# Hybrid attention/DeltaNet backbone, 1 core: attention in 32 units of two maps, products in halves of the array, seven modulation pairs moved into the first FFN

## What is computed

```python
s = einsum('bqhmd,bthmd->bhmqt', dq, dk) * 64**-0.5     # 4 differential heads, 2 maps each
p = softmax(s)
a = p[:, :, 0] - lam * p[:, :, 1]
d_out = rms_norm(einsum('bhqt,bthe->bqhe', a, dv), subln_g) * (1 - lam_init)
s = einsum('bqgrd,btgd->bgrqt', gq, gk) * 64**-0.5      # 8 grouped heads: 2 key heads, 4 queries each
g_out = einsum('bgrqt,btgd->bqgrd', softmax(s), gv)
y = concat(d_out, g_out) @ w_out
```

## Time and profile before

| | us |
|---|---|
| median of 3 runs | 1403.09 (1401.18 to 1406.2) |
| the profiled execution | 1406.29 |
| its span, first to last instruction | 1404.2 |
| mean granted TensorE clock | 0.939 of full |

### The profile page before, as it was taken

The page is one execution under the profiler, slowest core; times in us unless marked ns, Lnnn a source line. Parts: engine busy times, 40 slices in busy tenths (PEclk is TensorE's granted clock), DMA queues, the critical chain, the costliest instruction groups (busy, mean ns, idle before and its releaser), DMA issues.

```text
span 1404.2 us, 19657 instructions
## 1 busy us (share of the span) xinstructions
PE 1243.1 (89%) x7965; PEld 1013.4 (72%) x7965; DVE 664.8 (47%) x1016; ACT 573.0 (41%) x1003; POOL 183.4 (13%) x170
## 2 busy tenths in 40 slices
PE   5699989998949999999999579968758977999996
PEld 3377755566828888888888258867657966999996
DVE  2433257554373232333222564559955556555444
ACT  2322246444343222323222346555374635444542
POOL 0120320100041111111000310010011432111101
PEclk9899999999969999999999779988967999999998
DMA  7555555775303333333333112223101214466661
GB/s 280 180 166 152 163 165 180 240 255 151 90 15 91 90 105 91 100 95 88 93 107 87 36 45 71 66 75 93 29 1 41 54 31 120 138 186 186 172 182 40
DMA packets 239140, 159.63 MB, mean 114 GB/s; under 512 B 14522, under 2 KB 213580, under 8 KB 239052
## 3 DMA queue, kind: packets, MB, share of 16 engines
q1 hardware_dynamic: 238272, 158.10, 38.0%
q10 hardware_dynamic: 780, 0.29, 0.1%
HBM read 157.32 MB, written 1.05 MB: 113 GB/s over the span
## 4 chain that ended last, share of the span: by engine, by line
PE 76%; DVE 13%; ACT 5%; issue 2%; DMA 2%; POOL 1%; ACTq 0%; SPq 0%; DVEq 0%; POOLq 0%
PE bank L1331 55%; PE bank L1319 3%; PE bank L1456 2%; PE bank L1479 2%; PE bank L1370 2%; DVE w_lo L1736 2%; DVE h_lo L1783 1%; DVE xT L1806 1%; PE bank L1464 1%; PE bank L1301 1%; DVE blocks L995 1%; PE bank L754 1%; DVE outer L993 1%; DVE conv_out L1071 1%; DVE h_hi L1782 1%
## 5 line engine op out<-in xcount | busy, mean ns | idle before, releaser
L1331 PE MATMUL bank<-h_hi,w_hi 128*128 128x512 f32 (+2 forms) x1240 | 442.9, 357 | 63.5 <-DVE h_lo L1783 33.9
L1331 PE MATMUL bank<-h_lo,w_hi 128*128 128x512 f32 (+2 forms) x1240 | 434.7, 351 | 0.0
L1331 PE MATMUL bank<-h_hi,w_lo 128*128 128x512 f32 (+2 forms) x1240 | 434.2, 350 | 0.0
L1736 DVE TENSOR_TENSOR w_lo<-w_raw,w_hi 128x1024 fp32r<-128x1024 f32 (+1 forms) x203 | 249.8, 1232 | 307.1 <-ACT w_hi L1540 306.4
L1331 PEld LDWEIGHTS bank<-h_hi,w_hi 128*128 128x128 f32 (+1 forms) x1240 | 242.2, 195 | 105.5 <-issue 63.9
L1331 PEld LDWEIGHTS bank<-h_hi,w_lo 128*128 128x128 f32 (+1 forms) x1240 | 242.6, 196 | 29.7 <-issue 1.0
L1331 PEld LDWEIGHTS bank<-h_lo,w_hi 128*128 128x128 f32 (+1 forms) x1240 | 243.1, 196 | 27.0 <-issue 0.5
L1540 ACT ACTIVATE w_hi<-w_raw 128x1024 fp32r<-128x1024 f32 (+1 forms) x203 | 209.7, 1037 | 102.0 <-PE bank L1331 84.6
L1331 PE MATMUL bank<-act_hi,w_hi 128*128 128x512 f32 (+1 forms) x352 | 118.3, 336 | 0.0
L1331 PE MATMUL bank<-act_lo,w_hi 128*128 128x512 f32 (+1 forms) x352 | 118.3, 336 | 0.0
L1331 PE MATMUL bank<-act_hi,w_lo 128*128 128x512 f32 (+1 forms) x352 | 118.3, 336 | 0.0
(11 more groups left out here) (252 smaller groups left out, 1432.1 us busy)
## 6 DMA issues: line engine op xcount, KB each, us to landing
w_raw<-in_ada_w SPq DMA_DIRECT2D x96, 512.0 KB, 4.9
w_raw<-in_ffn_w_gate_up SPq DMA_DIRECT2D x88, 512.0 KB, 3.8
w_raw<-in_ffn_w_down SPq DMA_DIRECT2D x32, 512.0 KB, 4.0
w_raw<-in_gdn_w_in SPq DMA_DIRECT2D x32, 512.0 KB, 4.0
w_raw<-in_attn_w_in SPq DMA_DIRECT2D x14, 512.0 KB, 3.9
w_raw<-in_ffn_w_down SPq DMA_DIRECT2D x16, 384.0 KB, 3.3
w_raw<-in_attn_w_out SPq DMA_DIRECT2D x8, 512.0 KB, 4.9
w_raw<-in_gdn_w_out SPq DMA_DIRECT2D x8, 512.0 KB, 5.8
```

Of the source, the lines that this page charges most:

```text
L1331: m = nc.tensor.matmul(dst, stationary(a, k), moving(b, k), start=(first and k == kk[0] and a == b == 0), stop=(last and k == kk[-1] and a ...
L1736: nc.vector.tensor_tensor(w_lo[where[key] % N_RAW][:, 0:tiles, 0:w], raw_slot(key)[:, 0:tiles, 0:w], w_hi[m % N_SPLIT][:, 0:tiles, 0:w].bi ...
```

## The change

1. `ATT_UNITS` has 32 units, one of 8 tiles of 128 features and a block of 128 queries, each with two maps. Tiles 0 to 3 are the differential heads. Tiles 4 to 7 hold one grouped head of each key head.
2. `scores` gives each map the 64 rows of its own half: rows 0 to 63 and rows 64 to 127 of the array, into two banks. `q_sb` is no longer doubled, and POOL writes each query tile once.
3. `values` of a grouped tile puts each map's 64 value columns in its own half of the array's columns; the values are no longer doubled, and one copy takes the whole 128 partitions.
4. Attention has a ring of six banks ("att") and one bank for outputs ("out"); `o_stat` stays in "work".
5. Of the 31 modulation pairs 24 stay in attention (in every step but those with qb = 0), and 7 go behind the gate chunks n = 1, 3, ... 13 of the FFN of layer 0.
6. `SPLIT_OUT_AT` is n = 32, behind the last unit. Each chunk of the output projection comes in three DMAs, which sort its rows to the new order of heads.

```diff
-ATT_UNITS = [(head, qb) for head in range(DIFF_HEADS + GQA_HEADS) for qb in range(T // P)]
+ATT_UNITS = [(tile, qb) for tile in range(KT) for qb in range(T // P)]
...
+def key_tile(tile):
+    return 1 + tile if tile < DIFF_HEADS else 0
+
+
+def turned_maps(tile):
+    return range(1 if tile < DIFF_HEADS else 2)
...
-    if phase == "att" and step % 3 and ATT_PAIR[step] < 31:
-        return pair(34, ATT_PAIR[step])
+    if phase == "att" and step % 4:
+        return pair(34, step - step // 4 - 1)
+    if phase == "gate0" and step % 2 and step < 14:
+        return pair(82, step // 2)
...
-        q_sb = at("q_sb", [KT, 2, T], F32, BIG)
+        q_sb = at("q_sb", [KT, T], F32, BIG)
...
+        RINGS = {"work": (2, 3, 4, 5, 6), "side": (7, 1), "att": (2, 3, 4, 5, 6, 1), "out": (7,), "extra": (0, 7, 1), "core": (2, 3, 4, 5, 6, 7, 1, 0)}
...
                 for n in range(2 * FT):
                     project(("gate", layer, n), ("gate", layer, n), lo, i if n == 0 else None)
+                    ada(ada_after(f"gate{layer}", n))
...
             def scores(n):
...
+                tile, qb = ATT_UNITS[n]
+                if qb == 0:
+                    pe.wait_ge(qk_out, 5 + tile + 1)
+                dsts = [take(("s", n, m), "att") for m in range(2)]
+                for m in range(2):
+                    half = slice(m * HEAD, (m + 1) * HEAD)
+                    finish(nc.tensor.matmul(dsts[m][:, 0:keys_of(qb)], q_sb[half, tile, qb * P:(qb + 1) * P],
+                                            k_sb[half, key_tile(tile), 0:keys_of(qb)], start=True, stop=True),
+                           ("s", n, m))
...
             def turn(n):
...
+                for m in turned_maps(tile):
+                    dst = take(("t", n, m), "att")
+                    for t in range(keys_of(qb) // P):
+                        last = nc.tensor.transpose(dst[:, t * P:(t + 1) * P],
+                                                   probs[:, n % 3, m, t * P:(t + 1) * P], ident)
+                    finish(last, ("t", n, m))
...
             def values(n):
...
+                for t in range(tiles):
+                    if tile < DIFF_HEADS:
...
+                    for m in range(2):
+                        c0 = DIFF_HEADS * P + m * HEAD
+                        last = nc.tensor.matmul(dst[m * HEAD:(m + 1) * HEAD, qb * P:(qb + 1) * P],
+                                                v_sb[:, t, c0:c0 + HEAD], probsT[:, n % 2, m, t, :],
+                                                start=(t == 0), stop=(t == tiles - 1))
...
             def normalize(n):
...
-                if maps == 1:
-                    first.then_inc(probs_ready, 1)
+                if tile >= DIFF_HEADS:
+                    nc.vector.tensor_scalar(p[:, 1, :], p[:, 1, :], stats[:, n % 4, 5:6], None,
+                                            ALU.mult).then_inc(probs_ready, 1)
                     return
...
-                        for half in range(2):
-                            last = nc.gpsimd.tensor_scalar(q_sb[:, u - 5, half, :], qk_n[:, u % 3, :],
-                                                           tab[:, C_HALF + half:C_HALF + half + 1], one,
-                                                           ALU.mult, ALU.mult)
+                        last = nc.gpsimd.tensor_scalar(q_sb[:, u - 5, :], qk_n[:, u % 3, :], HEAD ** -0.5, None,
+                                                       ALU.mult)
...
+                elif key[0] == "attout":
+                    rest = attn_w_out[0][DIFF_HEADS * P:, key[1] * P:(key[1] + 1) * P]
+                    sp.dma_start(slot[:, 0:DIFF_HEADS, :],
+                                 columns(attn_w_out[0][0:DIFF_HEADS * P, :], key[1] * P)).then_inc(done, 16)
+                    for g in range(GQA_KV):
...
-SPLIT_OUT_AT = len(ATT_UNITS) - 4
+SPLIT_OUT_AT = len(ATT_UNITS)
```

More of the change, by code:

```diff
@@ L185, in stream @@
         for n in range(2 * FT):
-            out += [("gate", layer, n)]
+            out += [("gate", layer, n)] + [("ada", a) for a in ada_after(f"gate{layer}", n)]
         for m in range(KT):
@@ L1298, in turn_rows @@
                 pe.wait_ge(rows_ready, group + 1)
-                dst = take(("mod", group))
+                dst = take(("mod", group), "att" if group in ATT_GROUPS else "work")
                 for k in range(ADA_WIDTH // P):
@@ L1472, in values @@
                 if qb == 0:
-                    take(("o", head), "side")
-                dst = bank(("o", head))
-                wait_evacuated(pe, ("t", n))
-                c0 = head * P if head < DIFF_HEADS else 512 + (head - DIFF_HEADS) // 4 * P
+                    take(("o", tile), "out")
+                dst = bank(("o", tile))
+                for m in turned_maps(tile):
+                    wait_evacuated(pe, ("t", n, m))
                 tiles = keys_of(qb) // P
                 for t in range(tiles):
-                    m = nc.tensor.matmul(dst[:, qb * P:(qb + 1) * P], v_sb[:, t, c0:c0 + P],
-                                         probsT[:, n % 2, t, :], start=(t == 0), stop=(t == tiles - 1))
-                finish(m, ("v", n))
-                done_at[("o", head)] = jobs[0]
+                    if tile < DIFF_HEADS:
+                        last = nc.tensor.matmul(dst[:, qb * P:(qb + 1) * P], v_sb[:, t, tile * P:(tile + 1) * P],
+                                                probsT[:, n % 2, 0, t, :], start=(t == 0), stop=(t == tiles - 1))
+                        continue
+                    for m in range(2):
[3 more added lines that the diff above has]
+                                                start=(t == 0), stop=(t == tiles - 1))
+                finish(last, ("v", n))
+                done_at[("o", tile)] = jobs[0]
             for n in range(len(ATT_UNITS) + 4):
@@ L1883, in maxima @@
             def maxima(n):
-                head, qb = ATT_UNITS[n]
-                for m in range(len(maps_of(head))):
+                qb = ATT_UNITS[n][1]
+                for m in range(2):
                     wait_product(dve, ("s", n, m))
@@ L2092 @@
 LAST_QKV = ("qkv",) + QKV_STEPS[-1]
[L2093 removed]
+ATT_GROUPS = range(8, 20)
+SPLIT_OUT_AT = len(ATT_UNITS)
 SUBLN_AT = [4 * h + 7 for h in range(DIFF_HEADS)]
```

108 lines of the change are left out of this document (39 added, 69 removed).

## The result

The changed kernel takes 1391.21 us, the median of four runs (1388.32 to 1392.17), against 1404.64 for the kernel before (four runs, 1401.18 to 1406.68). The ratio is 0.9903 with a 95% interval of 0.9877 to 0.993, which leaves out 1: faster, by 1% or 13.4 us, where 1386.0 was forecast and the range was 1374 to 1400.

A forecast was written before the change was run, and what follows sets the result against it. PE was taken to bound the grouped heads and FFN, a fixed chain partly the differential heads. Terms -2.2, -1.3, -31.7, +5.3 and +12.6 sum to -17.3 us: 1389.0 profiled, 1386 median, range 1374 to 1400.

The forecast's parts named there:

- Do halves overlap: PE array: row and column halves overlap; a 64-row score pair takes 0.86 us (512 keys), a 64-column values pair 0.22.
- A change of shape, 0.11 us: PE, between products of different shape: each change costs 0.11 us, with bounds of 0.05 and 0.2.
- Start, -2.2: Start to first o_stat, 27.9 us before: query tiles written once save 1.7 us on POOL, faster scores 0.5.
- First to third o_stat, -1.3: Differential heads, 30.8 us before: the fixed chain of 6.33 us stays, each period takes 14.75 us.
- Third o_stat to last scores, -31.7: Grouped heads, 90.9 us before: four units take 14.2 us of PE work plus 0.5 of waits; 59.2 us in all.
- The end, +5.3: Attention's end, 7.6 us before: three ACT splits add 3.0 us, copies 1.2, a second maximum and exponential 1.1.
- The FFN, +12.6: FFN of layer 0: seven modulation pairs add 8.3 us, four turn_rows 3.5, a wait for DVE's copy 0.8.
- DVE and ACT: Rival, grouped heads: DVE and ACT become the bound, four units take 17 us, 9 more in all: 1395; chance 0.15.
- Passes in program order: Rival, PE: pairs of scores take three passes, +8 us: 1394; chance 0.06.
- no overlap: Rival, PE: the halves don't overlap at all, so +12.3 us: 1415; chance 0.05.
- The clock: Rival, attention: PE's waits make the clock fall again, some 3.5 us each, two falls: 1393; chance 0.07.
- more gain: Rival: the start doesn't fall to the low clock and the splits find room in ACT's waits: 1378; chance 0.12.

The follow-up runs named there:

- e1: Changed kernel with score products back on all 128 rows, each query tile written twice by POOL with one half zeroed: 1395.08 us.
- e2: Changed kernel with grouped values issued one column half after the other, not alternating: 1394.45 us.
- f4: Changed kernel with the differential heads' scaling one step later and scores on all 128 rows (e5 + e1): 1392.60 us.
- e4: Changed kernel with one output projection chunk split at attention's last step, not three: 1389.83 us.
- e6: Changed kernel with o_stat taking its bank from attention's own ring "att": 1385.71 us.
- e3: Changed kernel with the seven modulation pairs of the FFN back in attention: 1383.35 us.
- e5: Changed kernel with DVE scaling and splitting a differential head one step later, behind the next step's normalization: 1382.18 us.
- f2: Changed kernel with the later scaling and the seven modulation pairs back in attention (e5 + e3): 1382.17 us.
- f3: Changed kernel with the later scaling and o_stat in attention's ring (e5 + e6): 1377.78 us.
- e7: Changed kernel with three of the seven pairs in attention and four behind post_norm(0), in the norms' gap: 1390.56 us.
- f1: Changed kernel with four edits together (e3 + e4 + e5 + e6): 1378.79 us.

## Why the prediction was right, and where it was not

- **What bounds it.** Right: PE gave up 13.6 us of work, and the profiled execution fell by 14.1.
- **Do halves overlap.** Right, in rows and in columns, by e1, e2 and f4. For the columns they overlap in full if issued in turn, and for four of eight passes if not (e2).
- **A change of shape, 0.11 us.** Near: 16 changes in a period at 0.13 are the 2.0 us that 18 at 0.11 were. The period came out at 13.7 and not 14.7, since the 0.5 of waits weren't there and the period read above has one `turn_rows` where 1.5 were taken (0.44). The Trainium skill (TensorEngine Tiling (Array Packing), "Key Properties") has it that a change of tiling mode drains the engine; the timelines bear that out as a price of a fifth of a microsecond at most.
- **Start, -2.2: right by luck.** The term was "written once, half of both goes: 1.7 us", and POOL's writing gave 0.07. The shorter `scores`, for which the prediction took 0.5, gave more: e1, with full products and with the clock at half only at 183 us as in the changed kernel's profile, took 27.9 us where that took 25.7. The kernel before took 27.9 with a fall at 190 us; with such a fall the changed kernel, and those that do the same up to there (e2, e4, e6), take 28.5 to 28.8. So with the clock as it was before, the start did not get shorter, and its -2.2 belongs to an execution with a kinder clock. Why e1 without that fall is no faster there than before with it is open.
- **First to third o_stat, -1.3: this step failed.** It was +4.8. I wrote that the fixed chain stays and that "the two cheap `scores` inside the chain gain nothing", and stopped there. What PE no longer does inside a fixed chain becomes a wait; I had the rival that waits "in each period could make it fall again: some 3.5 us for each fall", and gave it 0.07. Four of five profiles with this wait had the fall, for 4.8 us (11.6 against 6.8); most of the rest of the 5.8 us by which 20.7 stands over e6's 14.8 is the wait of 0.84 for the bank. With both gone, e6 has 29.7 us for the two periods, 1.1 under before: so the chain and PE's work beside it were sized rightly, and the fall of the clock and the bank are what was left out. The list of what was "costed at nothing" left out that o_stat takes a bank from the ring of the turned maps.
- **Third o_stat to last scores, -31.7.** Measured -33.3.
- **The end, +5.3.** Measured +4.1: the splits' term was 3.0 and is 1.2 to 1.4 (e4).
- **The FFN, +12.6.** Measured +12.5, and e3 takes it back.
- **From the profiled execution to the median.** I took 3.2 us off, as before's lay above its median. The changed kernel's lay only 1.0 above. Of the 5.2 us between 1386.0 and 1391.2, this is 2.2 and the sum's error 3.2, less rounding.
- **The rivals.** DVE and ACT did not become the bound with the grouped heads: DVE was busy for 28.25 of 44 us there (262 to 306), 8.8 a period, where 10.7 was counted. Passes in program order and no overlap fell with e1 and e2. "The clock" happened in part, once, and so did "more gain": the clock stayed up at 190 us, and most of the splits lay beside work.

## What to carry to other kernels

When work is taken off the engine that bounds a kernel, look for chains of fixed length in which that work used to lie: there it turns into waits, and the first thing to try is the order of the items in the list of the engine waited for (e5: the scaling of a head one step later on DVE, 7.5 us). Measure the parts of a change again once the waits are gone: e3 and f2, e1 and f4 give the same edit 6 us and nothing, or 5 us and 10. When a piece of work is moved, count what comes along with it. And where a term of the sum comes out, look at its own rows all the same: the start's -2.2 stood beside a write on POOL that had not become shorter.

## What the runs showed of the hardware

- 64-row fp32 products in the two row halves run as one: 1.06 us a pair of 512 columns against 1.82 to 1.92 for two full ones. In column halves the same, if issued alternately: 1.03 us for sixteen of 128 columns, 1.78 for full ones. One half after the other takes 1.52: the second half's passes begin with the first's fifth, each half at the pace of full passes (0.11 us). For eight passes (four in each half) the order costs nothing, 0.60 against 0.58.
- A POOL multiplication of 128x512 fp32 by one constant took 1.49 us, one by two columns of a table 0.77 (most rows of each; before and e1 against after). What in the form makes the difference was not tried.
- Which falls of the clock come is not settled by a kernel's text: at 190 us, behind waits of 1.9 to 2.1 us, it stayed up in the changed kernel's first profile, f3 and f4 and fell in before, e3, e5, e7, f1 and f2. One fall costs 3 to 5 us, which is the size of the differences between edits here. What decides it is open.
